# Sums of q and k over heads in four column quarters, their spreads from four row quarters into four banks, and both at earlier places among the k and v products

## The reference, cut to what matters

```
def rms_norm_2(x, g=None):
    y = xf * lax.rsqrt(jnp.mean(xf * xf, axis=-1, keepdims=True) + EPS)
...
def qkv_heads(h, w_qkv, q_g, k_g):
    q, k, v = jnp.split(h @ w_qkv, 3, axis=-1)
    return rms_norm_2(_heads(q), q_g), rms_norm_2(_heads(k), k_g), _heads(v)
...
        q, k, v = qkv_heads(h, odd_w_qkv[i], odd_q_g[i], odd_k_g[i])
        q_c, k_c, v_c = qkv_heads(h_c, odd_w_qkv[i], odd_q_g[i], odd_k_g[i])
        y = _merge(neighbourhood_attention(q, k, v, k_c, v_c, odd_rpb[i])) @ odd_w_o[i]
```

## Time and profile before

| | us |
|---|---|
| three runs, median (lowest to highest) | 1710.36 (1709.32 to 1712.69) |
| the profiled execution, its own time | 1709.58 |
| its span in the trace | 1706.9 |
| PE busy | 1633.5 (96%) |
| DVE busy | 965.2 (57%) |
| ACT busy | 749.5 (44%) |
| chain that ended last, PE's share of the span | 76% |

### The profile page before, as it was taken

One profiled execution on the slowest core, in us unless ns is written; L12 is line 12 of the kernel. 1 busy time (PEld: TensorE's weight loads), 2 busy tenths in 40 slices (PEclk: granted clock), 3 DMA queues, 4 the chain that ended last, 5 costly groups with the idle time before them and its releaser, 6 DMA issues.

```text
span 1706.9 us, 27748 instructions
## 1 busy us (share of the span) xinstructions
PE 1633.5 (96%) x11819; PEld 1428.8 (84%) x11819; DVE 965.2 (57%) x1190; ACT 749.5 (44%) x1110; POOL 139.2 (8%) x103
## 2 busy tenths in 40 slices
PE   7999999999999999899979999999969999989998
PEld 6998998999989989887768888888859785779998
DVE  6887566568885565652455433443453226666674
ACT  5545545355555544642343331232243235655453
POOL 0320000003300000000020000000020101110000
PEclk9999999999999999999989999999979998989999
DMA  7775665776766658422113324322323323245764
GB/s 256 242 248 180 219 219 189 251 238 223 233 212 211 209 176 300 163 74 75 49 50 99 91 69 116 108 84 66 110 74 124 105 75 74 51 135 163 212 179 127
DMA packets 329948, 259.50 MB, mean 152 GB/s; under 512 B 24017, under 2 KB 322385, under 8 KB 329826
## 3 DMA queue, kind: packets, MB, share of 16 engines
q1 hardware_dynamic: 312002, 252.47, 46.7%
q10 hardware_dynamic: 17824, 5.27, 1.5%
HBM read 256.67 MB, written 1.05 MB: 151 GB/s over the span
## 4 chain that ended last, share of the span: by engine, by line
PE 76%; DVE 13%; ACT 6%; issue 2%; DMA 1%; POOL 1%; SPq 0%; DVEq 0%; ACTq 0%
PE banks_g L1109 37%; PE banks_g L810 16%; PE banks_g L800 4%; PE banks_g L1097 3%; DVE w_lo L1887 2%; PE banks_g L833 2%; DVE w_lo L2163 2%; ACT w_hi L1511 2%; PE banks_g L999 1%; ACT w_hi L1315 1%; PE bank_s L928 1%; PE banks_g L792 1%; PE bank_t L941 1%; ACT probs L1475 1%; POOL h L1825 1%
## 5 line engine op out<-in xcount | busy, mean ns | idle before, releaser
L1109 PE MATMUL banks_g<-h_hi,w_lo 128*128 128x512 f32 (+1 forms) x864 | 298.6, 346 | 9.7 <-DVE h_lo L2329 9.7
L1109 PE MATMUL banks_g<-h_lo,w_hi 128*128 128x512 f32 (+1 forms) x864 | 296.7, 343 | 0.0
L1109 PE MATMUL banks_g<-h_hi,w_hi 128*128 128x512 f32 (+1 forms) x864 | 296.6, 343 | 0.0
L2163 DVE TENSOR_TENSOR w_lo<-raw,w_hi 128x2048 fp32r<-128x2048 f32 (+1 forms) x100 | 207.7, 2077 | 155.9 <-ACT w_hi L1511 155.9
L1887 DVE TENSOR_TENSOR w_lo<-raw,w_hi 128x2048 fp32r<-128x2048 f32 x92 | 211.8, 2302 | 92.5 <-ACT w_hi L1315 92.4
L810 PE MATMUL banks_g<-h_hi,w_lo 128*128 128x256 f32 x800 | 227.7, 285 | 0.0
L810 PE MATMUL banks_g<-h_lo,w_hi 128*128 128x256 f32 x800 | 223.2, 279 | 0.0
L810 PE MATMUL banks_g<-h_hi,w_hi 128*128 128x256 f32 x800 | 223.2, 279 | 0.0
L1511 ACT ACTIVATE w_hi<-raw 128x2048 fp32r<-128x2048 f32 (+1 forms) x100 | 173.5, 1735 | 73.6 <-DMA raw<-w_down 47.4
L1109 PEld LDWEIGHTS banks_g<-h_hi,w_lo 128*128 128x128 f32 x864 | 164.8, 191 | 33.3 <-DVE h_lo L2329 12.0
L1315 ACT ACTIVATE w_hi<-raw 128x2048 fp32r<-128x2048 f32 x96 | 182.9, 1906 | 1.0 <-DMA raw<-w_branch 1.0
(11 more groups left out here) (357 smaller groups left out, 2902.0 us busy)
## 6 DMA issues: line engine op xcount, KB each, us to landing
raw<-w_in SPq DMA_DIRECT2D x76, 1024.0 KB, 5.1
ada_raw<-ada_w SPq DMA_DIRECT2D x48, 1024.0 KB, 7.4
raw<-w_up SPq DMA_DIRECT2D x88, 512.0 KB, 4.7
raw<-w_down SPq DMA_DIRECT2D x32, 704.0 KB, 4.4
raw<-w_branch SPq DMA_DIRECT2D x12, 1024.0 KB, 4.9
raw<-qkv SPq DMA_DIRECT2D x12, 1024.0 KB, 5.0
raw<-w_out SPq DMA_DIRECT2D x8, 1024.0 KB, 5.0
raw<-even_in SPq DMA_DIRECT2D x6, 1024.0 KB, 4.9
```

The source lines that it names most:

```text
L1109: last = nc.tensor.matmul(gb[:, m * SEQ:m * SEQ + nt], w[:, c, m0:m0 + P], a[:, c, 0:nt], start=c == 0 and n == 0, stop=c == kcs - 1 and n ...
L2163: nc.vector.tensor_tensor(w_lo[:, u % SLOTS, 0:n], raw[:, u % SLOTS, 0:n], w_hi[:, u % SLOTS, 0:n].bitcast(F32), ALU.subtract).then_inc(dv ...
```

## The change

1. **Sums in column quarters.** `head_sum` gets 32 columns (16 of them zero). Chunk c goes to columns 32(c mod 4) onward of the array, so to that quarter of the rows of `bank_m`; chunks 0 to 3 start the four quarters, 4 to 7 add to them. The root and the reciprocal are taken over 128 rows instead of 16.
2. **Spreads from row quarters.** `head_spread` lies on the row quarter of its chunk; chunk c reads rows 32(c mod 4) onward of `m_rstd` and writes one of four banks (two of `bank_s`, `bank_t`, `bank_o`). Spreads come in two halves of four; only the second half waits for DVE.
3. **Earlier places.** Both squares of q come right behind nq3, the rest as the new table says. The seven transfers move with the squares, the third bias load to "near exp 0".

```
-    t["head_sum"] = heads.astype(np.float32)
-    t["head_spread"] = np.ascontiguousarray(heads.transpose(2, 1, 0)).astype(np.float32)
+    head_sum = np.zeros((P, KC, 32), np.float32)
+    head_sum[:, :, 0:16] = heads
...
+    head_spread = np.zeros((P, 2, P), np.float32)
+    for ch in range(KC):
+        head_spread[32 * (ch % 4):32 * (ch % 4) + 16, ch // 4, :] = heads[:, ch, :].T
...
-    between = {"nk1": [("qk squares", "q", 0), ("qk squares", "q", 1)], "nk2": [("qk sum", "q", 0), ("qk sum", "q", 1)],
-               "nk3": [("qk spread", "q")], "nv0": [("qk squares", "k", 0)],
-               "nv1": [("qk sum", "k", 0), ("qk squares", "k", 1)], "nv2": [("qk sum", "k", 1)],
-               "nv3": [("qk spread", "k")]}
+    order += [("qk squares", "q", 0), ("qk squares", "q", 1)]
+    between = {"nk0": [("qk sum", "q", 0), ("qk sum", "q", 1)],
+               "nk1": [("qk spread", "q", 0), ("qk squares", "k", 0)],
+               "nk2": [("qk spread", "q", 1), ("qk sum", "k", 0)], "nk3": [("qk squares", "k", 1)],
+               "nv0": [("qk sum", "k", 1)], "nv1": [("qk spread", "k", 0)], "nv2": [("qk spread", "k", 1)]}
...
+        def spread_bank(c):
+
+            return [bank_s[:, 0:2, :].rearrange("p a k -> p (a k)"), bank_s[:, 2:4, :].rearrange("p a k -> p (a k)"),
+                    bank_t[:, :, :].rearrange("p a b -> p (a b)"), bank_o][c % 4]
...
-                        last = nc.tensor.matmul(bank_m[0:16, 0:nt], head_sum[:, c, :],
-                                                src[:, c % (8 if x == "q" else 4), :], start=c == 0, stop=c == KC - 1)
+                        r = slice(32 * (c % 4), 32 * (c % 4) + 32)
+                        last = nc.tensor.matmul(bank_m[r, 0:nt], head_sum[:, c, :],
+                                                src[:, c % (8 if x == "q" else 4), :], start=half == 0, stop=half == 1)
...
-                        if c >= 2:
-                            pe.wait_ge(dve_steps, dve_.at(f"normed{x}{c - 2}"))
-                        nc.tensor.matmul(dst, head_spread[0:16, c, :], m_rstd[0:16, 0:nt], start=True, stop=True
+                        r = slice(32 * (c % 4), 32 * (c % 4) + 32)
+                        if half:
+                            pe.wait_ge(dve_steps, dve_.at(f"normed{x}{c - 4}"))
+                        nc.tensor.matmul(spread_bank(c)[:, 0:nt], head_spread[r, half, :], m_rstd[r, 0:nt],
...
-                        pe.wait_ge(dve_steps, dve_.at(f"normedk{c}"))
+                        pe.wait_ge(dve_steps, dve_.at(f"normedk{max(c, 5)}"))
...
+                        act.wait_ge(dve_steps, dve_.at("h2 lo10 7"))
                         act.dma_start(head_sum[:, :, :], ins["head_sum"]).then_inc(odd_loaded, 16)
```

More of the change, by code:

```diff
@@ L100, in constants @@
     heads = (np.arange(16)[None, None, :] == 2 * np.arange(KC)[None, :, None] + (i // 64)[:, None, None])
-    t["head_sum"] = heads.astype(np.float32)
-    t["head_spread"] = np.ascontiguousarray(heads.transpose(2, 1, 0)).astype(np.float32)
+    head_sum = np.zeros((P, KC, 32), np.float32)
+    head_sum[:, :, 0:16] = heads
+    t["head_sum"] = head_sum
+    head_spread = np.zeros((P, 2, P), np.float32)
+    for ch in range(KC):
+        head_spread[32 * (ch % 4):32 * (ch % 4) + 16, ch // 4, :] = heads[:, ch, :].T
+    t["head_spread"] = head_spread
     col = np.arange(64)
@@ L523, in program @@
         q_n = sb("q_n", [P, KC, SEQ], offset=f_hi_at + 8192)
-        head_sum = sb("head_sum", [P, KC, 16], offset=f_hi_at + 16384)
-        head_spread = sb("head_spread", [16, KC, P], offset=f_hi_at + 16896)
+        head_sum = sb("head_sum", [P, KC, 32], offset=f_hi_at + 16384)
+        head_spread = sb("head_spread", [P, 2, P], offset=f_hi_at + 17408)
         qk_sq = sb("qk_sq", [P, 4, 512], offset=f_lo_at + 8192)
@@ L1188, in _ @@
                     for c in range(4 * half, 4 * half + 4):
-                        last = nc.tensor.matmul(bank_m[0:16, 0:nt], head_sum[:, c, :],
-                                                src[:, c % (8 if x == "q" else 4), :], start=c == 0, stop=c == KC - 1)
+                        r = slice(32 * (c % 4), 32 * (c % 4) + 32)
+                        last = nc.tensor.matmul(bank_m[r, 0:nt], head_sum[:, c, :],
+                                                src[:, c % (8 if x == "q" else 4), :], start=half == 0, stop=half == 1)
                     last.then_inc(pe_steps, pe_.step(f"sumsq{x}{half}"))
                 elif what == "qk spread":
-                    x, = arg
+                    x, half = arg
                     nt = SEQ if x == "q" else 512
                     pe.wait_ge(dve_steps, dve_.at(f"rstd{x}"))
-                    for c in range(KC):
-                        dst = (bank_t[:, :, :].rearrange("p a b -> p (a b)") if c % 2 == 0 else bank_o)[:, 0:nt]
-                        if c >= 2:
-                            pe.wait_ge(dve_steps, dve_.at(f"normed{x}{c - 2}"))
-                        nc.tensor.matmul(dst, head_spread[0:16, c, :], m_rstd[0:16, 0:nt], start=True, stop=True
-                                         ).then_inc(pe_steps, pe_.step(f"spread{x}{c}"))
+                    for c in range(4 * half, 4 * half + 4):
+                        r = slice(32 * (c % 4), 32 * (c % 4) + 32)
+                        if half:
+                            pe.wait_ge(dve_steps, dve_.at(f"normed{x}{c - 4}"))
+                        nc.tensor.matmul(spread_bank(c)[:, 0:nt], head_spread[r, half, :], m_rstd[r, 0:nt],
+                                         start=True, stop=True).then_inc(pe_steps, pe_.step(f"spread{x}{c}"))
                 elif what == "near scores":
@@ L1691, in _ @@
                     if (x, half) == ("q", 0):
+                        act.wait_ge(dve_steps, dve_.at("h2 lo10 7"))
                         act.dma_start(head_sum[:, :, :], ins["head_sum"]).then_inc(odd_loaded, 16)
[L1694 removed]
+                        act.dma_start(head_spread[:, :, :], ins["head_spread"]).then_inc(odd_loaded, 16)
                         act.dma_start(window[:, :], ins["window"]).then_inc(odd_loaded, 16)
@@ L1712, in _ @@
                         by, e_ = (1.0, eps_hd) if x == "q" else (1.0 / HD, eps)
[L1713 to L1717, removed]
+                        nc.scalar.activation(m_root[:, 0:nt], bank_m[:, 0:nt], ACT.Sqrt, scale=by,
+                                             bias=e_[:, 0:1]).then_inc(act_steps, act_.step(f"root{x}"))
+                elif what == "near exp":
+                    b, = arg
+                    if b == 0:
                         act.wait_ge(pe_steps, pe_.at(f"job{END_JOBS[('nv', 3, 1)]}"))
                         load_bias(2)
-                elif what == "near exp":
-                    b, = arg
                     if b >= 2 and b % 2 == 0 and b // 2 + 2 < 8:
@@ L2365, in _ @@
                         own()
-                        nc.vector.reciprocal(m_rstd[0:16, 0:nt], m_root[0:16, 0:nt]).then_inc(
+                        nc.vector.reciprocal(m_rstd[:, 0:nt], m_root[:, 0:nt]).then_inc(
                             dve_steps, dve_.step(f"rstd{x}"))
                 elif what == "qk spread":
-                    x, = arg
+                    x, half = arg
                     nt = SEQ if x == "q" else 512
-                    for c in range(KC):
+                    for c in range(4 * half, 4 * half + 4):
                         dst = (q_n if x == "q" else k_n)[:, c, :]
                         n = ROWS[x + "_g"]
-                        src = (bank_t[:, :, :].rearrange("p a b -> p (a b)") if c % 2 == 0 else bank_o)[:, 0:nt]
+                        src = spread_bank(c)[:, 0:nt]
                         dve.wait_ge(pe_steps, pe_.at(f"spread{x}{c}"))
```

## The result

| | before | changed |
|---|---|---|
| median of four runs each (lowest to highest), us | 1711.53 (1709.32 to 1714.23) | 1689.45 (1686.51 to 1691.42) |
| the profiled execution, its own time | 1709.58 | 1686.51 |
| its span | 1706.9 | 1684.7 |

The changed kernel takes 0.9871 of the time before, 95% interval 0.9857 to 0.9886: 22.1 us less (by the interval 19.5 to 24.5), where 22.3 were forecast, and 1689.45 where 1688.1 stood, inside the range. In the changed kernel the lines are moved: sums L1201, spreads L1213, k products L1120, v products L1108, near scores L1227.

The account below looks back on a forecast made before the run. PE bounds the kernel, busy 1633.5 of 1706.9 us. Won 27.8 (steps before) + 1.4 + 1.0 = 30.2, paid 3.0 + 3.8 + 0.4 + 0.7 = 7.9, net 22.3: 1710.36 to 1688.1 us, range 1684.6 to 1692.8.

Parts of the forecast that it names:

- three sums: The sum of q and two half sums of k, in column quarters, would take 1.0 us each, 3.0 together.
- four half spreads: Spreads from row quarters: 0.7 us per half for q, 1.2 for k, together 3.8; bounds 2.6 and 10.4.
- clock behind the spread of q: The first 17 v matmuls would run at full clock, with the stalls for DVE gone: 1.4 us won.
- first near scores at full clock: The first near scores would find the full clock, 1.06 us instead of 2.03: 1.0 us won.
- wait for ACT's last copy: At the end of nv3, near scores must wait until ACT has emptied their bank: 0.7 us lost.
- two more places between units: Sums and spreads stand in six places between units; going in and coming out of two more costs 0.4 us.
- rival of quarters one after the other: Row quarters don't run side by side; spreads cost 10.4 us instead of 3.8, kernel 1694.7 us; chance 0.10.
- Drain: A change of tiling mode drains the engine; dearer than 0.2 us, it would show as longer gaps at all six places.
- Early squares: Squares of q behind nq3 end just before PE's sum of q, 0.6 us in hand: cost nothing, thinnest cover.
- The slower rival: Near scores never regain the clock; sixteen blocks grow 2.0 us each, 10 us slower than before, 1720 us; chance 0.02.
- nothing won or lost there: Behind the first near scores the clock can fall as before; counted zero, at best 0.65 us and as much again.
- The third bias: Its load loses cover as near scores start 10 us sooner; windowing ends before DVE's first use, 2 us in hand.

Follow-up runs that it names:

- tiles_only: Against the kernel before: sums in column quarters and spreads from row quarters into four banks, all at the old places; 17.2 us faster, ratio 0.9893.
- the late wait: Changed kernel with the near scores' wait for ACT's last v copy before block 1 instead of 0; two runs, 24.4 and 23.8 us faster than before.
- sums_only: Against the kernel before: only sums in column quarters, at old places, spreads one after the other in two banks; 10.1 us faster, ratio 0.9946.
- the spreads alone: Changed kernel with sums one by one again as full 128-column products, spreads unchanged; 15.7 us faster than before, ratio 0.9910.
- one_row: New places and four banks without wait within a half, but sums one by one and spreads all from the same 16 rows; 3.8 us faster than before.
- places_only: Changed kernel's order, but sums and spreads one by one on 16 rows, two banks with waits for DVE; 0.6 us faster than before, ratio 0.9983.
- two_banks: Changed kernel with row quarters writing alternately into two banks, waiting for DVE from a half's third matmul on; 10.2 us faster than before, ratio 0.9934.
- held_squares: Changed kernel with three more squares of q on ACT between the seven transfers and the real squares; 18.4 us faster than before, ratio 0.9890.

## Why the prediction was right, point by point

| term | forecast | measured |
|---|---|---|
| steps before | 27.8 | the rows themselves |
| three sums | 3.0 | 1.00 + 0.99 + 0.99 = 3.0 |
| four half spreads | 3.8 (2.6 to 10.4) | 2 x 0.64 + 2 x 1.07 = 3.4 |
| clock behind the spread of q | 1.4 | 24.33 - 22.81 (tiles_only, same place) = 1.5 |
| first near scores at full clock | 1.0 | start to DVE's first add: before 2.2, after 1.2 |
| wait for ACT's last copy | 0.7 | 0.85, by the late wait |
| two more places between units | 0.4 | what is left: 0.4 |
| net | 22.3 | 22.6 in the stretch, 22.1 in the median |

*Sums.* The `ada` product was the right model, 1.00 for 1.00; the runs for the sums alone and for the spreads alone put the part's worth at 7.6 and 7.35.

*Spreads.* The step "0.20 for the second tile, 0.07 for each further one" was too dear: four quarters cost 1.07, no more than the pair of halves with 1.06, as their matmuls start 0.01 us apart. The Trainium skill, "TensorE: Matmul & The Clock Gate", Why this matters for your kernels, gives 3.07x for four tiles of 32 rows and 512 columns; the trace has 4 x 0.86 / 1.07 = 3.2x. By the page's figure a half of k would have been 3.44 / 3.07 = 1.12, an estimate. My rival of quarters one after the other is refuted, and one_row shows what it would have looked like.

*Drain.* "TensorEngine Tiling (Array Packing)" of the Trainium skill, Key Properties, names a drain at each change of tiling mode; it does no more here than what the transitions cost before. The sum of q starts 0.32 us behind the last product (1313.10 to 1313.42), as it did before (0.33).

*The clock.* The term was right, 1.4 for 1.5, the reason wrong; that it came out is luck in part. I held that the falls come of the stops for DVE. They come as well behind spreads that never stop (one_row), and none came behind a spread of q that does stop (tiles_only). What the runs show is where falls stood: behind the whole spread of q, and within that of k, on one row quarter or in two banks (before, sums_only; q 6.16 and 4.87 us, k at a granted clock of 0.65), behind the first half of k wherever it took 4.0 to 5.2 us (places_only, one_row, two_banks), behind the second half, at 3.6 to 3.9 us, in one of these three (places_only), and never behind halves in four tiles at once, 1.1 us at most, nor behind halves of q of up to 2.3 us. A consequence that I had missed: the new places without the tiles lose most of what they win. Also, I leaned on 96 `ada` products that leave the clock up; the trace has 48 of them (768 matmul records, 16 to a product), which changes nothing in the argument.

*Early squares.* Right: nothing waits for them. In the timeline of ACT of the changed kernel the transfers hold it 1302.34 to 1310.95 = 8.6 us instead of 8.2:

```profile
1302.34 0.60 ACT L1629 ACTIVATE q_n<-banks_g 128x512 f32<-128x512 f32 x1 [3.25 <-PE banks_g L1120]
...
1310.95 2.15 ACT L1719 ACTIVATE qk_sq<-q_n 128x1024 f32<-128x1024 f32 x2 [8.01 <-issue]
```

The squares end at 1313.10 and PE starts the sum at 1313.42, 0.3 us apart where I had 0.6. But that comparison wasn't the one that counts: the first half of the sum needs only the first square, ended by 1312.0 (two in 2.15 us), and the second half starts half of 1.00 later. With 0.14 from ACT to PE (held_squares) there are 1.3 us in hand for the first half and, as an estimate, 0.7 for the second; in the run with the squares held, what lay beyond came through to PE and lowered the clock besides.

*The slower rival.* It needed near scores that stay at the low clock. They fall for about 4 us at most, in some profiles and not in others (0.64 over 4.8 us in the changed kernel). The fall was there in all three profiles of the changed kernel, so the term "nothing won or lost there" came out with some luck: without the fall the change would have won 1.6 us more.

*The third bias.* Its windowing ends 1408.66 + 2.36 = 1411.0 by POOL's timeline, 11.7 us behind the end of nv3, before DVE's first use at 1413.33 in its timeline: 2.3 us in hand for the 2 forecast.

## What to carry to other kernels

A short matmul with a small side, in the path of a dense engine, is worth its whole length: price it by the start-to-start distance in the chain, and look for a tiled form elsewhere in the same trace as its model. Give row quarters a bank each, so that they needn't wait for its reader, and find the reader a place to hide; of the 22.6 us the tiles gave 17.65, the places 4.9 more on top, but by themselves only 2.85, of which 0.3 up to the near scores. Moving a step forward also moves the transfers in front of it: count how long they hold their engine, here 8.6 us, with about 1 us in hand.

## What the runs showed that I had not expected

The granted clock fell to 0.50 behind four spreads of k one by one, 3.9 us in which PE was busy throughout, and not behind the next four, 3.7 us of the same (one_row). It never fell behind sums of 3.5 us that use all rows and 16 columns. What sets spreads apart from sums is open, the rows used being one candidate that no run here isolates; and what sets the two halves of k apart, which are the same matmuls, is open as well. Two profiles of one program differ by 1.6 us through a fall in the near scores that one has and the other hasn't, so a single profile can't judge an edit of that size. And of the versions run, the late wait is a little better than the changed kernel: 0.85 us in the trace, in both of its profiles.
